# Differential attention in a two-layer decoder: q's swapped rows by ScalarE copies, the output norm's factor by Ln and Exp

## What is computed

```python
def apply_rope(x, cos, sin):                 # x [B,T,H,2,64]
    x1, x2 = split(x, 2, -1)
    return concatenate([x1 * cos - x2 * sin, x2 * cos + x1 * sin], -1)

def diff_attention(x, ...):                  # 8 heads, each with two maps of width 64 and values of width 128
    q, k, v = split(x @ w_in, 3)
    q, k = apply_rope(q), apply_rope(k)
    s = einsum(q, k) * 64 ** -0.5            # causal, two maps c = 0, 1 per head
    p = softmax(s); p = p[:, :, 0] - lam * p[:, :, 1]
    o = p @ v
    o = rms_norm(o, subln_w) * (1.0 - lambda_init)   # o * rsqrt(mean(o*o) + 1e-6) * w, over 128 columns
    return o @ w_out
```

## Time and profile before

| | |
|---|---|
| median of 3 runs | 1406.9 us (1406.07 to 1408.09) |
| profiled execution, its own time | 1406.08 us |
| its span | 1404.3 us |
| PE busy | 1376.3 us, 98% |
| PEld busy | 1134.5 us, 81% |
| DVE busy | 868.5 us, 62% |
| ACT busy | 639.8 us, 46% |
| POOL busy | 70.7 us, 5% |
| granted TensorE clock | 0.998, all slices at 9 tenths or more |

### The profile page before, as it was taken

One profiled execution on the slowest core, in us unless ns is written; L12 is line 12 of the kernel. 1 busy time (PEld: TensorE's weight loads), 2 busy tenths in 40 slices (PEclk: granted clock), 3 DMA queues, 4 the chain that ended last, 5 costly groups with the idle time before them and its releaser, 6 DMA issues.

```text
span 1404.3 us, 19981 instructions
## 1 busy us (share of the span) xinstructions
PE 1376.3 (98%) x7038; PEld 1134.5 (81%) x7038; DVE 868.5 (62%) x1374; ACT 639.8 (46%) x1041; POOL 70.7 (5%) x86
## 2 busy tenths in 40 slices
PE   8899999999999999999999999999999999999997
PEld 7688888888788888888888876766898888888886
DVE  4677777777486666666326547777677666664226
ACT  5676656666324444443222346566334444443111
POOL 3100000000000000000000011111000000000002
PEclk9999999999999999999999999999999999999999
DMA  6212212121223333333323311221223333343231
GB/s 204 60 53 69 69 45 52 53 68 60 61 61 90 90 104 90 105 108 128 120 90 105 91 45 46 60 75 45 91 61 91 104 92 102 90 132 122 90 105 60
DMA packets 157731, 118.92 MB, mean 85 GB/s; under 512 B 5898, under 2 KB 145644, under 8 KB 157676
## 3 DMA queue, kind: packets, MB, share of 16 engines
q1 hardware_dynamic: 157676, 118.17, 28.1%
HBM read 116.04 MB, written 2.11 MB: 84 GB/s over the span
## 4 chain that ended last, share of the span: by engine, by line
PE 91%; DVE 5%; ACT 2%; DMA 1%; issue 1%; SPq 0%; DVEq 0%; ACTq 0%
PE bank L1693 13%; PE bank L1694 13%; PE bank L1695 13%; PE bank L1708 11%; PE bank L1681 8%; PE bank L1683 8%; PE bank L1682 8%; PE bank L1770 3%; PE bank L2092 2%; PE bank L1768 1%; PE bank L2110 1%; PE bank L1777 1%; PE bank L2053 1%; PE bank L1659 1%; PE bank L1786 1%; PE bank L2104 1%
## 5 line engine op out<-in xcount | busy, mean ns | idle before, releaser
L375 DVE TENSOR_TENSOR w_lo<-raw,w_hi 128x1024 fp32r<-128x1024 f32 x188 | 230.1, 1225 | 223.8 <-ACT w_hi L364 205.8
L1693 PE MATMUL bank<-x_hi,w_hi 128*128 128x512 f32 (+1 forms) x912 | 347.2, 381 | 2.6 <-DVE x_lo L1061 1.9
L1695 PE MATMUL bank<-x_hi,w_lo 128*128 128x512 f32 (+1 forms) x912 | 340.0, 373 | 0.0
L1694 PE MATMUL bank<-x_lo,w_hi 128*128 128x512 f32 (+1 forms) x912 | 339.8, 373 | 0.0
L364 ACT ACTIVATE w_hi<-raw 128x1024 fp32r<-128x1024 f32 x176 | 184.6, 1050 | 153.1 <-PE bank L1683 130.4
L1693 PEld LDWEIGHTS bank<-x_hi,w_hi 128*128 128x128 f32 x912 | 171.9, 189 | 33.6 <-DVE x_lo L1061 2.4
L1695 PEld LDWEIGHTS bank<-x_hi,w_lo 128*128 128x128 f32 x912 | 171.7, 188 | 30.3
L1694 PEld LDWEIGHTS bank<-x_lo,w_hi 128*128 128x128 f32 x912 | 172.0, 189 | 29.4 <-issue 1.4
L1681 PE MATMUL bank<-w_hi,u_hi 128*128 128x512 f32 x416 | 163.8, 394 | 0.6 <-DVE w_lo L375 0.6
L1683 PE MATMUL bank<-w_hi,u_lo 128*128 128x512 f32 x416 | 162.0, 389 | 0.0
L1682 PE MATMUL bank<-w_lo,u_hi 128*128 128x512 f32 x416 | 161.9, 389 | 0.0
(11 more groups left out here) (292 smaller groups left out, 1991.3 us busy)
## 6 DMA issues: line engine op xcount, KB each, us to landing
raw<-in_ffn_w_up SPq DMA_DIRECT2D x88, 512.0 KB, 3.8
raw<-in_ffn_w_down SPq DMA_DIRECT2D x44, 512.0 KB, 3.4
raw<-in_gdn_w_in SPq DMA_DIRECT2D x32, 512.0 KB, 4.1
raw<-in_diff_w_in SPq DMA_DIRECT2D x24, 512.0 KB, 3.7
raw<-in_gdn_w_out SPq DMA_DIRECT2D x8, 512.0 KB, 3.5
raw<-in_diff_w_out SPq DMA_DIRECT2D x8, 512.0 KB, 3.4
x_tok<-in_x SPq DMA_DIRECT2D x4, 512.0 KB, 5.6
ROW<-decay_rows SPq DMA_DIRECT2D x8, 256.0 KB, 4.6
```

Source lines behind the costliest of these rows:

```text
L375: nc.vector.tensor_tensor(w_lo[:, s, :], raw[:, (base + r) % RAW, :], w_hi[:, s, :].bitcast(F32), ALU.subtract).then_inc(lo_ready, 1)
L1693: nc.tensor.matmul(out, hi, x_hi[:, k, cols], start=(k == 0), stop=False)
L1694: nc.tensor.matmul(out, hi, x_lo[:, k, cols], start=False, stop=False)
L1695: ins = nc.tensor.matmul(out, lo, x_hi[:, k, cols], start=False, stop=last)
```

## The change

- q is no longer rotated on TensorE. ScalarE copies the four blocks of 32 rows of q's bank, exchanged and with their signs, into `rope2[0]` (`swapped`); it stands between turned_p 2 and turned_p 3, where the weight split stood, and the split comes behind turned_p 3. Ahead of head 0 it follows the copy of q. VectorE multiplies `rope2[0]` by `sin` in place.
- The bank of q is given free by `swapped`, no longer by `take`; GpSimd's product with `cos` waits for a semaphore of its own, `q_taken`.
- VectorE does rope of q ahead of split_lo.
- The factor of the norm becomes Exp(-0.5 Ln(z)). VectorE makes z and a flag with four small operations (`ranged`) behind the sum of squares, and `row_factor` is one multiplication that stands behind maxima 0.
- The table set is loaded by name ahead of head 0 and named again ahead of each Ln.

```diff
@@ GpSimd
             def rope_cos(g, kind):
-                wait_read(pool, kind, T_QK // 2 + g)
+                if kind == 0:
+                    pool.wait_ge(q_taken, g + 1)
+                else:
+                    wait_read(pool, kind, T_QK // 2 + g)
@@ ScalarE
+            def swapped(g):
+                if not (isinstance(g, int) and g == 0):
+                    act.wait_ge(rope_head, R_DVE0 + RD_N * (g - 1) + RD["qr"])
+                for b in range(4):
+                    src, dst = slice(32 * (b ^ 1), 32 * (b ^ 1) + 32), slice(32 * b, 32 * b + 32)
+                    ins = nc.scalar.activation(rope2[0][dst, :], bank[0][src, :], ACT.Copy,
+                                               scale=HD ** -0.5 * (1.0 if b % 2 else -1.0))
+                ins.then_inc(bank_read[0], 1)
...
                 turned_p(2)
                 if more:
-                    split_hi(act, C_QK, it, 2 * r + 5)
+                    swapped(h + 1)
...
                 turned_p(3)
+                if more:
+                    split_hi(act, C_QK, it, 2 * r + 5)
...
-                nc.scalar.activation(att_sq[:, :], att_o[:, :], ACT.Square, scale=P ** -0.5).then_inc(n_act, 1)
-                act.wait_ge(n_dve, ND_N * h + ND["ms"])
-                nc.scalar.activation(att_rms[:, 1, :], att_rms[:, 0, :], ACT.Sqrt, bias=bias_rms_small,
-                                     scale=SMALL * SMALL).then_inc(n_act, 1)
+                nc.scalar.activation(att_sq[:, :], att_o[:, :], ACT.Square, scale=SMALL * P ** -0.5).then_inc(n_act, 1)
+                nc.scalar.preload_act_table_set("natural_log_exp_and_others")
+                act.wait_ge(n_dve, ND_N * h + ND["z"])
+                nc.scalar.activation(att_rms[:, 1, :], att_rms[:, 3, :], ACT.Ln).then_inc(n_act, 1)
+                act.wait_ge(n_act, NA_N * h + NA["ln"])
+                nc.scalar.activation(att_rms[:, 1, :], att_rms[:, 1, :], ACT.Exp, scale=-0.5).then_inc(n_act, 1)
@@ VectorE
             def rope(g, kind):
-                dve.wait_ge(rot_pe, 2 * g + kind + 1)
-                nc.vector.tensor_tensor(rope2[kind][:, :], bank[4 + kind][:, :], sin[:, :], ALU.mult).then_inc(rope_head, 1)
+                if kind == 0:
+                    wait_read(dve, 0, T_QK // 2 + g)
+                    nc.vector.tensor_tensor(rope2[0][:, :], rope2[0][:, :], sin[:, :], ALU.mult).then_inc(rope_head, 1)
+                else:
+                    dve.wait_ge(rot_pe, g + 1)
+                    nc.vector.tensor_tensor(rope2[1][:, :], bank[5][:, :], sin[:, :], ALU.mult).then_inc(rope_head, 1)
...
             def row_factor(h):
-                nc.vector.reciprocal(rstd, rstd).then_inc(n_dve, 1)
-                n_own(h, "inv")
-                nc.vector.scalar_tensor_tensor(rstd, ms, F32_MAX / P, rstd, ALU.is_le, ALU.mult).then_inc(n_dve, 1)
+                n_own(h, "fl")
+                nc.vector.tensor_tensor(rstd, rstd, att_rms[:, 4, :], ALU.mult).then_inc(n_dve, 1)
+            def ranged(h):
+                ms, g, z, fl = (att_rms[:, i, :] for i in (0, 2, 3, 4))
+                n_own(h, "ms")
+                nc.vector.tensor_scalar(g, ms, 2.0 ** 40, 2.0 ** -72, ALU.is_le, ALU.max).then_inc(n_dve, 1)
+                n_own(h, "g")
+                nc.vector.scalar_tensor_tensor(z, ms, RMS_EPS * SMALL * SMALL, g, ALU.add, ALU.mult).then_inc(n_dve, 1)
+                nc.vector.tensor_scalar(fl, ms, 2.0 ** 40, 2.0 ** -36, ALU.is_le, ALU.max).then_inc(n_dve, 1)
+                n_own(h, "root")
+                nc.vector.scalar_tensor_tensor(fl, ms, F32_MAX / P * SMALL * SMALL, fl, ALU.is_le,
+                                               ALU.mult).then_inc(n_dve, 1)
...
                 rope(h, 1)
+                maxima(0)
                 if not first:
                     row_factor(h - 1)
-                maxima(0)
...
                 mix(3)
                 if more:
+                    rope(h + 1, 0)
                     split_lo(dve, C_QK, it, 2 * r + 5)
-                    rope(h + 1, 0)
...
                 nc.vector.tensor_reduce(att_rms[:, 0, :], ...)
+                ranged(h)
@@ TensorE
                 values(2)
-                if not last:
-                    rotate(h + 1, 0)
                 turn(3)
```

More of the change, by code:

```diff
@@ L198, in build @@
         small = sb("small", [P, 16])
-        eps = sb("eps", [P, 3])
+        eps = sb("eps", [P, 2])
         lamv = sb("lamv", [P, 4, HD])
@@ L256, in build @@
         att_sq = place("ul", 8, "att_sq", [P, T])
-        att_rms = place("ul", 9, "att_rms", [P, 2, NT])
+        att_rms = place("ul", 9, "att_rms", [P, 5, NT])
         att_o = place("ul", 10, "att_o", [P, T])
@@ L316, in build @@
         t_pe, t_dve, t_act, v_head = sem("t_pe"), sem("t_dve"), sem("t_act"), sem("v_head")
+        q_taken = sem("q_taken")
         rot_pe, rope_pool, rope_head = sem("rot_pe"), sem("rope_pool"), sem("rope_head")
@@ L348, in build @@
         bias_ln = eps[:, 1:2]
-        bias_rms_small = eps[:, 2:3]
         rows_dram = nc.dram_tensor("decay_rows", (HEADS, T), F32, kind="Internal").ap()
@@ L969, in take @@
                     act.wait_ge(rope_pool, 2 * g + kind - 1)
-                nc.scalar.activation(qk_raw[kind][:, :], bank[kind][:, :], ACT.Copy,
-                                     scale=(HD ** -0.5 if kind == 0 else 1.0)).then_inc(bank_read[kind], 1)
+                ins = nc.scalar.activation(qk_raw[kind][:, :], bank[kind][:, :], ACT.Copy,
+                                           scale=(HD ** -0.5 if kind == 0 else 1.0))
+                ins.then_inc(*((q_taken, 1) if kind == 0 else (bank_read[1], 1)))
+            def swapped(g):
[6 more added lines that the diff above has]
+                ins.then_inc(bank_read[0], 1)
             def step(it, r):
@@ L1030, in _ @@
             take(0, 0)
+            swapped(0)
             split_hi_after(act, C_QK + 3, C_V)
@@ L1047, in _ @@
             nc.vector.memset(eps[:, 0:1], RMS_EPS)
-            nc.vector.memset(eps[:, 2:3], RMS_EPS * SMALL * SMALL)
             nc.vector.memset(small[:, :], 0.0)
@@ L1551, in row_factor @@
             def row_factor(h):
-                ms, rstd = att_rms[:, 0, :], att_rms[:, 1, :]
+                rstd = att_rms[:, 1, :]
                 dve.wait_ge(n_act, NA_N * h + NA["std"])
-                nc.vector.reciprocal(rstd, rstd).then_inc(n_dve, 1)
-                n_own(h, "inv")
-                nc.vector.scalar_tensor_tensor(rstd, ms, F32_MAX / P, rstd, ALU.is_le, ALU.mult).then_inc(n_dve, 1)
+                n_own(h, "fl")
[10 more added lines that the diff above has]
+                                               ALU.mult).then_inc(n_dve, 1)
             def scaled_out(h):
@@ L2048, in project_qk, with rotate_k @@
                     block_products(kind, (C_QK + 2 * odd + kind) % WS, k, k == KT - 1)
-            def rotate(g, kind):
-                wait_read(pe, kind, T_QK // 2 + g)
-                nc.tensor.matmul(bank[4 + kind][:, :], swap[:, :], qk_raw[kind][:, :], start=True,
+            def rotate_k(g):
+                wait_read(pe, 1, T_QK // 2 + g)
+                nc.tensor.matmul(bank[5][:, :], swap[:, :], qk_raw[1][:, :], start=True,
                                  stop=True).then_inc(rot_pe, 1)
@@ L2117, in step @@
                 if not first:
-                    rotate(h, 1)
+                    rotate_k(h)
                 fill(1, 3)
@@ L2153, in _ @@
             pe.wait_ge(v_out, 2 * (NT - 1))
-            rotate(0, 0)
             v_unit(NT - 1, HELD)
-            rotate(0, 1)
+            rotate_k(0)
             for k in range(HELD + 1, KT):
@@ L2197 @@
 RD, RD_N = numbered(["rope2 q", "qr", "rope2 k", "kr"])
-ND, ND_N = numbered(["oc", "ms", "inv", "flag", "o", "lo"])
-NA, NA_N = numbered(["sq", "std", "hi"])
+ND, ND_N = numbered(["oc", "ms", "g", "z", "root", "fl", "flag", "o", "lo"])
+NA, NA_N = numbered(["sq", "ln", "std", "hi"])
 D_DVE0 = 1 + DVE_N
```

## The result

The changed kernel takes 1416.03 us, median of four runs (1415.07 to 1418.03), against 1406.49 for the kernel before in the same comparison. The ratio is 1.0067, with a 95% interval of 1.0053 to 1.0082. It is slower by 9.5 us, outside the predicted range (1404.7 to 1410.8). The profiled execution took 1415.07 us with a span of 1413.3 us: 9.0 us more span than before.

A forecast was written before the change was run, and what follows sets the result against it. TensorE, busy 98% of 1404.3 us, was taken to bound the kernel. Seven turns of -0.86 + 0.61 + 0.32 + 0.20 = +0.27 us (+1.9) and -0.86 ahead of head 0 gave +1.0 us: 1407.9 us, range 1404.7 to 1410.8.

The forecast's parts named there:

- one ladder: Turn of the head, from k's copy on ScalarE to the scores: chain of 3.28 us, said to have no slack on VectorE.
- q's rotation: TensorE's chain in heads 0 to 6 and ahead of head 0: leaving TensorE, it saves 0.86 us each time.
- The four small operations: VectorE, between the reduction and k's sine product: said to add 0.61 us a turn (0.45 to 0.85).
- the clash: GpSimd's copy of vh holds z, the second small VectorE operation: +0.32 us a turn; rival without it 0.26.
- One table load stays in each head: Rival on ScalarE: a table load remains per head, costs nothing, time as forecast; no separate chance given.
- Four copies late, on the Square: ScalarE's copies of q's rows: 1.96 us in all, Square on time by 0.03 us, so no cost.
- Factor behind the maxima: VectorE, one multiplication between maxima and scaling: +0.20 us on TensorE in each of heads 1 to 7 (0.1 to 0.25).
- my dear bound: Upper bound for ScalarE's four copies of q's rows: 2.4 us with no overlap, instead of 1.96.
- a Square 0.3 us late: Rival of late copies on ScalarE: clash goes, time again 1407.9 us; chance 0.46 together with the forecast.
- the hold for z alone: Only the second small VectorE operation was charged a wait for GpSimd's copy: 0.32 us, bounds 0 and 0.52.
- E: Moment when ScalarE starts to copy k out of its bank: said to come 0.86 us earlier in each of seven heads.
- TensorE's wait: Wait of the score weights for k's sum at the head's turn: said to grow from 0.56 to about 1.5 us.

The follow-up runs named there:

- q's part alone: Changed kernel with the norm as before; only swapped rows, copies and the split's move stay: 1403.24 us, ratio 0.9976 to the kernel before.
- the loop written out: norm's part alone with GpSimd's copy of vh ahead of its k product, and VectorE's heads 1 to 6 without a loop: 1411.82 us, single run.
- norm's part alone: Changed kernel with q's rotation left on TensorE and the split in its old place; only the norm's new form stays: 1416.99 us, ratio 1.0074.
- the kernels with the clamp first: q's part alone with VectorE's clamp of att_o ahead of its half of the split: 1401.92 us; further edits were made on it.

## Why the prediction was wrong

**What held.** The place was right: one ladder, without slack, sets the turn. q's rotation brought -0.88 us ahead of head 0 and, in q's part alone, -0.88 us in a regular head (-0.86 said). The four small operations cost what was said without the clash: k's product 1.30 us behind the reduction in the loop written out, 1.28 said. An operation that doesn't wait follows after 0.08 us (916.98 to 917.06), as worked out from a single pair of rows. The clash exists, 0.35 against 0.32 us. One table load stays in each head (915.87, by the named load, although the set is in place), a rival that was costed at nothing; it ends at 917.15, and nothing waits for it.

**Terms that were mis-sized**, for a regular turn:

| Term | Said | Measured |
|---|---|---|
| q's rotation (q's part alone) | -0.86 | -0.88 |
| Four copies late, on the Square | 0 | +0.40 |
| Four small operations and clash | +0.61 + 0.32 | +0.80 |
| Factor behind the maxima (norm's part alone) | +0.20 | +0.13 |
| k's sum behind its product | 0 | +0.09 |
| Turn | +0.27 | +0.55 |

The copies are the first cause. I took 0.49 us each from a row of a full copy and let partitions not count; they cost 0.60 us each, my dear bound. The prediction named what follows, a Square 0.3 us late, but then let it cancel with the clash ("the clash goes; this ends at the forecast again"). It didn't cancel. The late ladder moved the clash from z to the first small operation (916.60, 0.34 us; it takes 0.16 us where GpSimd is idle, with `ranged` behind k's products) and left 0.17 us of it, so 0.40 + 0.17 stood where 0.32 was said. I had priced the hold for z alone, which has two SBUF inputs. The Trainium skill, page SBUF — State Buffer, section Who interferes with whom, says that tensor_scalar, too, can take the port pair shared with GpSimd, in its two-port modes; 0.34 against 0.16 us beside GpSimd's copy agrees with it, and so does the 0.94 us of L1621.

The 0.09 us goes with a wait value that differs by one between k's product and its sum. It is gone where both wait for the same value and in head 7, which is written out (0.71 to 0.73 us); my reading is that VectorE computes the value in between. Most of it is not lost, though: in q's part alone k's product starts 0.61 us behind the reduction instead of 0.67, so that the two distances sum to 1.42 us, against 1.40 before. The factor behind the maxima makes the scaling 0.18 us late, as said, the transposes 0.06 us and E 0.13 us.

**A term that was missing.** The end of VectorE's loop costs 0.42 us at two of the turns, 0.84 us in all. The kernel before has the same loop and shows no extra (0.67 us in every turn); my reading, which no run isolates, is that the reduction of 0.69 us as last operation of the body covers it there, and four short operations don't.

**The step that failed.** Seven turns with 0.55 us, the loop's ends, and -0.77 us ahead are 3.85 + 0.84 - 0.77 = +3.9 us. The other 5 us are not in any term. The prediction let TensorE's wait grow from 0.56 to 1.5 us and charged the wait alone. The runs showed that TensorE's idling has a price behind it: after three of seven such waits the granted clock was 1.2 instead of 2.4 GHz for about 3 us. That slows the fill work, and delays VectorE's third Pm by 1.41 us and GpSimd's product by 1.24 us, so that they meet; I had seen this in head 0 and counted it as a fact of head 0. Together they are 2.06 us in each of two turns, and the last fall accounts for most of the 0.96 us behind the last S. Filling the same wait with useless matmuls took 4.6 us off. Where the wait was 0.6 us or less (q's part alone), the clock stayed full. The clock is not the whole miss: with it full the kernel took 1411.41 us, 3.5 us above the forecast and 0.6 us above the range, and that part is the ladder's, by the table and the loop's ends.

**The two halves.** Alone they are -3.3 and +10.5 us, +7.2 together, and the full change is +9.5. The traces differ in the falls of the clock, three in the full change and one in the norm's part alone; that these make up the 2.3 us is an inference. With the four small operations moved, both together are -2.1 us. So the norm's new form is not what costs: its place ahead of k's product is, with 10.9 us. Of the kernels here the fastest is q's part alone with the clamp ahead of the split, GpSimd's q product behind the third Pm and one wait value: 1399.93 us, 7.4 us under before; the last of these edits is not clear of noise.

**Open.** Why the clock fell after a wait of 1.40 us at 986.73 and not after 1.84 at 941.12 isn't settled; the wait alone doesn't decide it, in the norm's part alone neither (1.59 and 1.60 us). That GpSimd's copy holds k's sum in the kernel with one wait value (0.77 us, the copy beside it from 888.62) was not tested by an edit of its own, but the traces speak for it: in the kernels with the clamp first the sum starts 2.54, 2.60 or 2.64 us behind E and always ends at 3.36 to 3.38. The held Pm and the half clock were not taken apart by a run: filling the wait removed both.

## What to carry to other kernels

Where an engine's wait grows, price what comes after the wait, too: the clock behind it, and each pair of operations that now meet (a margin of 0.2 us between VectorE's product and GpSimd's was all that kept them apart in the regular heads, and delays of 1.41 and 1.24 us used it up). Small operations belong behind the one that another engine waits for, even if they take 0.16 us each. And when two of your bounds would each shift the same ladder, add them up in time, step by step, before you let one cancel the other.

## What the runs showed that was not expected

- The granted clock of TensorE can halve 1.1 to 1.7 us after a wait of 1.4 to 1.9 us in an otherwise full stretch (0.50 from 897 to 899 us). It did so behind three of seven such waits here and one of seven (1.14 to 1.60 us) in the norm's part alone, behind none of seven of 0.79 to 1.25 us, and with the wait filled it stayed at 1.00.
- ScalarE's copies of 32 rows between different row blocks follow each other after 0.60 us; copies that begin at the first row follow each other after 0.48 us (885.99 to 886.47).
- Operations of 128x4 on VectorE are held by GpSimd like large ones: 0.51 against 0.16 us with two SBUF inputs, 0.34 against 0.16 us with one.
- The end of a loop cost VectorE 0.41 to 0.47 us where the operations ahead of it are short, and a wait value that changes between k's product and its sum put them 0.09 us further apart.
- Naming the table set in each head issued a load of 1.28 us in each (8 loads at L1035), though no other set had been loaded since head 0.
